# Gates as feature tiles between the attention's chunks, applied behind the outputs' transposes

## The reference

```
z = rmsnorm(x, n1) @ w_in             # 1024 -> [u | q | f | i | gate], 512 each
y_pool = (window means of u, minus u) @ w_pool * scale     # 4 groups, windows 2,4,8,16
q = silu(q) * 128**-0.5;  log_f, k from f and lb;  v = i    # 4 heads of 128
o = S-recurrence over chunks: causal part with decays + q * exp(G) @ S
o = o * rsqrt(mean(o*o) + eps) * g_norm * silu(gate)
x = x + concat(y_pool, o) @ w_out
x = x + conv_ffn(rmsnorm(x, n2));  y = final rmsnorm
```

## Time and profile before

| | us |
|---|---|
| median of 3 runs | 2874.8 (2872.68 to 2878.28) |
| the profiled execution | 2871.09 |
| its span, first to last instruction | 2869.2 |
| PE busy in the span | 2614.6 (91%) |
| DVE busy | 1202.9 (42%) |
| ACT busy | 697.0 (24%) |
| POOL busy | 440.4 (15%) |
| mean granted clock of TensorE | 0.955 of full |

### The profile page before, as it was taken

One profiled execution on the slowest core, in us unless ns is written; L12 is line 12 of the kernel. 1 busy time (PEld: TensorE's weight loads), 2 busy tenths in 40 slices (PEclk: granted clock), 3 DMA queues, 4 the chain that ended last, 5 costly groups with the idle time before them and its releaser, 6 DMA issues.

```text
span 2869.2 us, 34984 instructions
## 1 busy us (share of the span) xinstructions
PE 2614.6 (91%) x12479; PEld 2132.6 (74%) x12479; DVE 1202.9 (42%) x2344; ACT 697.0 (24%) x1389; POOL 440.4 (15%) x316
## 2 busy tenths in 40 slices
PE   5977786999889998899999998899999998899997
PEld 4865665888767787688877787688877787688776
DVE  5624844444524548422224548321224746322224
ACT  2211302222222333211122323211122422211123
POOL 3420332455545102000000002000000011000000
PEclk8986898999989999999999999899999999999999
DMA  4542023666666651355564641355555631355553
GB/s 146 192 160 88 8 97 113 225 237 220 237 224 230 254 209 45 118 185 188 188 217 181 238 173 44 121 189 190 189 221 193 246 125 60 147 190 190 209 194 137
DMA packets 142288, 489.07 MB, mean 170 GB/s; under 512 B 8897, under 2 KB 75697, under 8 KB 92840
## 3 DMA queue, kind: packets, MB, share of 16 engines
q1 hardware_dynamic: 133689, 482.67, 47.1%
q10 hardware_dynamic: 8472, 4.75, 0.6%
HBM read 375.54 MB, written 112.02 MB: 170 GB/s over the span
## 4 chain that ended last, share of the span: by engine, by line
PE 64%; DMA 8%; DVE 6%; issue 4%; ACT 2%; SPq 1%; DVEq 0%; POOL 0%; ACTq 0%
PE ps L493 20%; PE ps L495 20%; PE ps L494 20%; DMA w_split<-w_both 8%; PE ps L621 1%; DVE arena L1647 1%; PE ps L647 1%; ACT arena L972 1%; SPq L370 1%; DVE arena L1615 1%; PE ps L525 0%; DVE x_tok L1709 0%; DVE arena L1614 0%; DVE h_lo L1367 0%; DVE arena L1359 0%
## 5 line engine op out<-in xcount | busy, mean ns | idle before, releaser
L493 PE MATMUL ps<-h_hi,w_both 128*128 128x512 f32 (+1 forms) x1888 | 746.9, 396 | 19.2 <-DVE x_tok L1709 8.9
L495 PE MATMUL ps<-h_lo,w_both 128*128 128x512 f32 (+1 forms) x1888 | 739.2, 392 | 0.0
L494 PE MATMUL ps<-h_hi,w_both 128*128 128x512 f32 (+1 forms) x1888 | 736.0, 390 | 0.0
L493 PEld LDWEIGHTS ps<-h_hi,w_both 128*128 128x128 f32 x1888 | 360.7, 191 | 97.6 <-issue 21.8
L495 PEld LDWEIGHTS ps<-h_lo,w_both 128*128 128x128 f32 x1888 | 360.4, 191 | 81.5
L494 PEld LDWEIGHTS ps<-h_hi,w_both 128*128 128x128 f32 x1888 | 361.1, 191 | 78.8
L493 PE MATMUL ps<-w_both,act_hi 128*128 128x512 f32 (+1 forms) x748 | 301.2, 403 | 27.2 <-DVE act_lo L1782 27.2
L495 PE MATMUL ps<-w_both,act_hi 128*128 128x512 f32 (+1 forms) x748 | 299.2, 400 | 0.0
L494 PE MATMUL ps<-w_both,act_lo 128*128 128x512 f32 (+1 forms) x748 | 298.3, 399 | 0.0
L1782 DVE TENSOR_TENSOR act_lo<-arena,act_hi 128x512 fp32r<-128x512 f32 (+1 forms) x176 | 133.5, 762 | 342.9 <-ACT act_hi L1255 342.9
L328 POOL TENSOR_TENSOR arena<-arena 128x256 f32<-128x256 f32 x56 | 40.5, 723 | 1511.8 <-DVE arena L1615 1511.8
(11 more groups left out here) (238 smaller groups left out, 2924.0 us busy)
## 6 DMA issues: line engine op xcount, KB each, us to landing
w_both<-w_split SPq DMA_DIRECT2D x288, 1024.0 KB, 4.8
w_split<-w_both SPq DMA_DIRECT2D x96, 1024.0 KB, 6.2
w_raw<-in_w_down SPq DMA_DIRECT2D x24, 512.0 KB, 4.2
w_raw<-in_w_a SPq DMA_DIRECT2D x22, 512.0 KB, 4.3
w_raw<-in_w_b SPq DMA_DIRECT2D x22, 512.0 KB, 4.3
w_raw<-in_w_in SPq DMA_DIRECT2D x20, 512.0 KB, 4.3
x_tok<-in_x_prompt SPq DMA_DIRECT2D x16, 512.0 KB, 6.7
arena<-in_x_prompt SPq DMA_DIRECT2D x16, 512.0 KB, 5.6
```

Source lines behind the costliest of these rows:

```text
L493: nc.tensor.matmul(out, lhs[0], rhs[0], start=first, stop=False)
L494: nc.tensor.matmul(out, lhs[1], rhs[0], start=False, stop=False)
L495: return nc.tensor.matmul(out, lhs[0], rhs[1], start=False, stop=last)
```

## The change

The order of the units becomes f, q, v, u, gate. V's token tiles go to PSUM banks 4 to 7, in the place of the gates. The gates are now feature tiles of 24 matmuls (`gate_tile`), in banks 6 and 7 by turns. In blocks 1 to 3 they lie behind chunks 5, 7, 8 and 10, and u tiles 1 to 3 behind chunks 0, 2 and 4. In block 0 gate tile 0 comes ahead of the attention, the others behind chunks 2, 6 and 10, with their head rows in bank 4, which the outputs use: so PE waits there for ACT's copy (`gate_taken`) ahead of the next outputs. `u_tile(0)` now waits for ACT's copies of v (`v_taken`), since they free bank 6.

ACT copies each gate tile from PSUM over the sums of logarithms `g_t`, when the last decays have read them (`take_gate`, wait on `eg_ready`). It applies SiLU to them in place behind chunks 10 to 13, with a table load for Silu behind chunk 9 and one back behind chunk 13.

The outputs are no longer multiplied by the gate in the chunk. ACT copies them from PSUM to `o_tok`, then squares from there; PE waits for that copy alone (`o_taken`). The pooled products go behind chunks 12 to 15, in block 0 too, where their head rows (bank 4) again make PE wait for the low part (`pool_taken`) before it goes on; the output product waits for all four.

In the tail DVE scales `o_tok` by the root alone, PE transposes it, and DVE multiplies the transposes by the gain (now a column of `vec`) and the gate tile into `yg` (`gated`); ACT's high and DVE's low part read `yg`. The load of the gain over all partitions is gone.

```diff
-U_F, U_Q, U_GATE, U_V, U_U, U_OUT, U_UP, U_DOWN = 0, 4, 8, 12, 16, 20, 28, 72
+U_F, U_Q, U_V, U_U, U_GATE, U_OUT, U_UP, U_DOWN = 0, 4, 8, 12, 16, 20, 28, 72
-U_BEHIND = {g: g + 1 for g in range(HEADS - 1)}
-POOLED_BEHIND = {0: 0, 1: 1, 2: 2, 11: 3}
-PRODUCT_BEHIND = {10 + g: g for g in range(HEADS)}
-LOW_BEHIND = {11 + g: g for g in range(HEADS)}
+U_BEHIND = {0: 1, 2: 2, 4: 3}
+POOLED_BEHIND = {0: 0, 1: 1, 3: 2, 10: 3}
+GATE_BEHIND = ({5: 0, 7: 1, 8: 2, 10: 3}, {2: 1, 6: 2, 10: 3})
+SILU_BEHIND = {10: 0, 11: 1, 12: 2, 13: 3}
+PRODUCT_BEHIND = {12 + g: g for g in range(HEADS)}
+LOW_BEHIND = ({13: (0,), 14: (1,), 15: (2, 3)}, {12 + g: (g,) for g in range(HEADS)})
```

PE in `attention`, its waits ahead of a chunk's outputs, what it puts behind a chunk, and the new `gate_tile`:

```diff
-                        pe.wait_ge(o_squared, n)
-                        pe.wait_ge(o_gated, n)
+                        pe.wait_ge(o_taken, n)
+                    if hd and i == 0:
+                        pe.wait_ge(gate_taken, 1)
+                    if hd and i - 1 in GATE_BEHIND[1]:
+                        pe.wait_ge(gate_taken, GATE_BEHIND[1][i - 1] + 1)
+                    if hd and i - 1 in PRODUCT_BEHIND:
+                        pe.wait_ge(pool_taken, PRODUCT_BEHIND[i - 1] + 1)
...
+                    if i in GATE_BEHIND[hd]:
+                        gate_tile(b, hd, GATE_BEHIND[hd][i], i + 1)
+                    if i in PRODUCT_BEHIND:
+                        pool_product(b, hd, PRODUCT_BEHIND[i], i + 1)
...
+            def gate_tile(b, hd, g, chunks):
+                if g < 2:
+                    pe.wait_ge(u_taken, 4 * b + (4 if hd else 3 + g))
+                else:
+                    pe.wait_ge(gate_taken, 4 * b + g - 1)
+                feature_tile(b, U_GATE + g, g, 6 + g % 2, 4, hd, win(2 + g % 2).start, chunks)
```

PE in `body`, ahead of the attention:

```diff
-                token_tiles(b, U_GATE, (4, 5, 6, 7), 2, hd)
+                token_tiles(b, U_V, (4, 5, 6, 7), 2, hd)
...
-                token_tiles(b, U_V, (0, 1, 2, 3), 4, hd)
-                pe.wait_ge(gate_taken, 4 * b + 4)
...
-                    for g in range(HEADS):
-                        pe.wait_ge(pooled_ready, g + 1)
...
-                    pe.wait_ge(pool_taken, 4)
...
+                    gate_tile(0, 1, 0, 0)
                 attention(b, hd)
```

ACT:

```diff
+                def take_gate(g):
+                    act.wait_ge(unit_done, UNITS * b + U_GATE + g + 1)
+                    act.wait_ge(eg_ready, 4 * b + g + 1)
...
+                    nc.scalar.copy(gate_t[:, g, HEAD:WIDE], ps[:, 6 + g % 2, :]).then_inc(gate_taken, 1)
+                def silu(g):
+                    act.wait_ge(gate_taken, 4 * b + g + 1)
+                    nc.scalar.activation(gate_t[:, g, lo:WIDE], gate_t[:, g, lo:WIDE], ACT.Silu).then_inc(gate_ready, 1)
...
                     act.wait_ge(o_done, n + 1)
+                    nc.scalar.copy(o_tok[:, w, win(h)], ps[:, 4, 0:P]).then_inc(o_taken, 1)
+                    act.wait_ge(o_taken, n + 1)
...
+                    if i == min(SILU_BEHIND) - 1:
+                        nc.scalar.preload_act_table(ACT.Silu)
```

DVE in the attention and in the tail (`mixer_output`):

```diff
-                    dve.wait_ge(o_squared, n + 1)
-                    v.tensor_tensor(gt, gt, ps[:, 4, 0:P], ALU.mult).then_inc(o_gated, 1)
...
-                        last = v.scalar_tensor_tensor(out=gt, in0=gt, scalar=orstd[rows, 4 * t + h:4 * t + h + 1],
-                                                      in1=gn[rows, :], op0=ALU.mult, op1=ALU.mult)
+                        last = v.tensor_scalar(ot, ot, orstd[rows, 4 * t + h:4 * t + h + 1], None, ALU.mult)
...
+                    v.scalar_tensor_tensor(out=yg[:, t, :].rearrange("p (k n) -> p k n", k=4),
+                                           in0=ps[:, 6 + t % 2, :].rearrange("p (k n) -> p k n", k=4), scalar=gcol,
+                                           in1=gate_t[:, :, main(t)], op0=ALU.mult, op1=ALU.mult).then_inc(yg_ready, 1)
```

More of the change, by code:

```diff
@@ L201, in trunk_step @@
         g_t = part(4480, HEADS, WIDE)
-        gate = part(6720, TILES + 1, 512)
+        o_tok = part(6720, TILES + 1, 512)
+        gate_t = g_t
         v_tok = part(9280, TILES + 1, 512)
@@ L540, in feature_tile @@
                 if hd:
-                    last = features(u % 4, ps[:, bank_head, 0:HEAD], slice(0, HEAD))
+                    if o_behind:
+                        pe.wait_ge(o_taken, o_behind)
+                    last = features(u % 4, ps[:, bank_head, at:at + HEAD], slice(0, HEAD))
                 last.then_inc(unit_done, 1)
@@ L673, in u_tile, with pool_product @@
                     pe.wait_ge(u_taken, 4 * b + g - 1)
+                else:
+                    pe.wait_ge(v_taken, 4 * b + 3 + g)
                 feature_tile(b, U_U + g, g, 6 + g % 2, None, 0)
-            def pool_product(b, g):
+            def gate_tile(b, hd, g, chunks):
+                if g < 2:
+                    pe.wait_ge(u_taken, 4 * b + (4 if hd else 3 + g))
+                else:
+                    pe.wait_ge(gate_taken, 4 * b + g - 1)
+                feature_tile(b, U_GATE + g, g, 6 + g % 2, 4, hd, win(2 + g % 2).start, chunks)
+            def pool_product(b, hd, g, chunks):
                 pe.wait_ge(pooled_ready, 4 * b + g + 1)
-                if g >= 2:
+                if g < 2:
+                    pe.wait_ge(gate_taken, 4 * b + 3 + g)
+                else:
                     pe.wait_ge(pool_taken, 4 * b + g - 1)
-                nc.tensor.matmul(ps[:, 6 + g % 2, :], wp[:, g, :], pooled[:, g, HEAD:WIDE], start=True,
-                                 stop=True).then_inc(pool_done, 1)
+                last = nc.tensor.matmul(ps[:, 6 + g % 2, :], wp[:, g, :], pooled[:, g, HEAD:WIDE], start=True, stop=True)
+                if hd:
+                    at = win(2 + g % 2).start
+                    pe.wait_ge(o_taken, chunks)
+                    last = nc.tensor.matmul(ps[:, 4, at:at + HEAD], wp[:, g, :], pooled[:, g, 0:HEAD], start=True,
+                                            stop=True)
+                last.then_inc(pool_done, 1)
             def head_attention():
@@ L803, in body @@
                     if t >= 2:
[L804 removed]
+                        pe.wait_ge(yg_ready, 4 * b + t - 1)
                     for h in range(HEADS):
[L806 removed]
+                        last = nc.tensor.transpose(ps[:, 6 + t % 2, h * P:(h + 1) * P], o_tok[:, t, h * P:(h + 1) * P], ident)
                     last.then_inc(yt_done, 1)
@@ L1664, in attention @@
                                            in1=ps[:, 5, P:2 * P], op0=ALU.mult, op1=ALU.add).then_inc(s_ready, 1)
-                    gt = gate[:, w, win(h)]
-                    dve.wait_ge(o_squared, n + 1)
-                    v.tensor_tensor(gt, gt, ps[:, 4, 0:P], ALU.mult).then_inc(o_gated, 1)
-                    if not hd and i in LOW_BEHIND:
-                        pool_low(b, hd, LOW_BEHIND[i])
+                    for g in LOW_BEHIND[hd].get(i, ()):
+                        pool_low(b, hd, g)
                     if not hd and i in POOLED_BEHIND:
```

132 lines of the change are left out of this document (64 added, 68 removed).

## The result

The change made the kernel **slower**: 2887.07 us (2883.47 to 2887.8, 6 runs) against 2876.19 (2872.68 to 2880.72, 6 runs) of the kernel before, ratio 1.0033, 95% interval 1.0021 to 1.0045. That is 10.9 more; the forecast was 3.6 less, and the range ended at 2886.0.

What follows compares the result with a forecast made beforehand. The prediction took TensorE as the bound, busy for 2614.6 of 2869.2 us. Block 0's -13.5 and +9.9 for blocks 1 to 3 (+3.3 each) gave -3.6, a median of 2871.2 us, range 2857 to 2886.

Steps and rivals of the forecast that it cites:

- V's gap: Blocks 1 to 3, ahead of attention: PE idles 4.5, outputs start 17.6 us earlier, clock costs 1.6; together -16.0 a block.
- 99.2, chunk 5 in 10, chunk 10 in 10.5: Block 1's attention: expected durations in us; the attention of blocks 1 to 3 was priced at +18.0 each.
- +1.3: Tail of blocks 1 to 3: eight DVE passes instead of four delay PE's second half to 6.05 us, +1.3 a block.
- Rival 2: Slower: TensorE's clock falls to 1.2 GHz at eight more new or longer waits, 1.6 each, 2884.0 us; chance 0.17.
- -13.5: Block 0 in all: gates and v, head recurrence, stretch ahead of attention, attention and tail sum to 13.5 us less.
- Head recurrence -2.8: Block 0's four heads: DVE's wait for ACT's square and its gate multiplication go, 0.7 us each, -2.8 (0 to -8).
- Ahead of the attention -9.5: Block 0: four serial products go; transposes, gate tile 0 and copies replace them, 26.0 us instead of 35.5.
- Attention +23.2: Block 0: gate tiles behind chunks 2 and 6 +9.1 and +7.5, chunk 10 0, catch-up -4.1, products +10.7 us.
- Tail +2.1: Block 0's tail: 1.3 us for the added DVE passes and 0.8 for the head rows' serial gate pass.
- rival 4: Block 0: PE waits for gate units split by slow POOL, losing 4 to 13.5 us, 2875.2 to 2884.7; chance 0.10.
- Rival 3: The Silu table load costs more than its 1.28 us row; if double, 1.28 more at four chunks 10, 2876.3; chance 0.03.
- Rival 1: Faster: tiles fill the attention's idle in blocks 1 to 3, floor +12.5, 5.5 us less a block, 2854.7; chance 0.25.

Runs made afterwards that it cites:

- Six repairs together: Changed kernel with earlier v copies, reordered ScalarE work (attention and block 0), head-row products together, early transposes, table padded to 128 rows: 2823.24 us, ratio 0.9818 to before.

## Why the prediction was wrong

**Blocks 1 to 3: the sum right, its terms in part by luck.**
- V's gap: forecast idle 4.5, start 17.6 earlier, 1.6 of clock; measured 4.36, clock 0.59. Right, and here the clock fell in all three blocks; the run with the gap filled shows the clock's price apart from the wait's.
- Attention, "99.2, chunk 5 in 10, chunk 10 in 10.5": 97.4, 9.7 and 9.9. The waits are where they were said, by the reasons that were said (the run with the other order on ScalarE), each 0.3 to 0.6 smaller. Chunk 3's 6.0 had the same cause; I took it for the kernel's own, and it was the largest of the three, 2.8.
- Tail, "+1.3", 6.05 said and 6.12 measured. Here **the clock was left out**: it fell behind the tail in all three blocks. That its 1.6 to 2 a block made up for the attention's 1.8 is luck, and so is the last row of the table above.
- Rival 2, with a chance of 0.17, named eight new places for this. The clock fell at four: the three tails, and block 0's last product (0.59 in the 4 us behind it). Behind chunk 10's wait of 1.6 it stayed at 1.00 in all of blocks 1 to 3, and in block 0 chunk 10 holds less idle time than before (2.0, and 7.9 before).

**Block 0: -13.5 said, +6.6 measured.** The steps that failed are the head recurrence and the stretch ahead of the attention (together 8.0 over their forecast), the tail (4.5), the attention (3.3), and two terms put at nothing without a reason, the clock behind the tail (2.5) and the start (2.4):
- The start, left out of the sum and so taken at 0: 2.4 by one more row in a table. I had read this part of the change as costing nothing.
- "Head recurrence -2.8": +0.9. VectorE's saved wait is there (intervals of 25.0 are 24.1 to 24.7 now, some 2.1 in all). But PE is busy for 16.3 and not 19.3 in two of the four intervals before and in one after, as the clock falls less there, which is 3.0. In the kernel with 113 rows, otherwise like before, the same stretch took 91.3 and not 88.3. So the term was about right, and the profile before had a lucky clock.
- "Ahead of the attention -9.5": -5.2. A split of a gate unit by GpSimd stands beside VectorE's last pooling sums there now: four of them take 5.64 where they took 2.90 (rows below), and PE waits 6.45 for the state work behind them, where before 3.9. And gate tile 0 took 11.2, not 9.4. The larger point is that I priced this tile as serial with the decays and didn't ask why: the order on ScalarE made it so (13.4 in the run). Together with the head recurrence this was forecast at -12.3 and is -4.3. Against two other profiles of the order before (129.7 and 132.8, where this one has 127.7) it would be -6.3 and -9.4; the changed order takes 122.6 to 123.5 in eight profiles. So a part of this miss is the execution that was profiled before.
- "Attention +23.2": +26.5. Chunks 2 and 6 took 12.3 and 12.4 as said, the four products' stretch 21.9 (22.2 said). Chunk 10 took 14.2, 2.4 more and not 0, near the upper bound of 2.7 named there. Light chunks gave back 3.1, not 4.1.
- "Tail +2.1": +6.6, of which 2.9 because two low parts from SBUF met GpSimd's split (4.19, and 1.29 before). The earlier trace rows had shown that pairing, and rival 4 named it for another place. The other 1.6 is the clock behind the last product's wait.
- Behind the tail 0, measured +2.5. The clock in that window is 0.89 and was 0.96.

VectorE's pooling sums ahead of block 0's attention, before and after, and GpSimd's split beside the latter:

```profile
269.13 2.90 DVE L1482 TENSOR_TENSOR arena<-arena 128x526 f32<-128x526 f32 x4
```

```profile
245.33 5.64 DVE L1516 TENSOR_TENSOR arena<-arena 128x526 f32<-128x526 f32 x4
247.76 2.66 POOL L478 TENSOR_TENSOR w_both<-w_raw,w_both 128x1024 fp32r<-128x1024 f32 x1
```

Rival 3 was wrong. ACT at chunk 9 and 10 of block 1:

```profile
1128.47 1.28 ACT L1165 ACT_TABLE_LOAD   x1
1129.77 0.27 ACT L1144 COPY arena<-ps 128x128 f32<-128x128 f32 x1
```

The kd copy starts as the load ends; nothing drains, and the drain that the Trainium skill, "ScalarE: Activation LUTs", section "What ACT_TABLE_LOAD costs", gives has no row here. Rival 1 was refused by the chunks, and the reason given against it was right. Rival 4's waits for split units are not there: PE waited 0.2 for them in all.

**What stays open.** Of the 16.8 between the profiles a part is the clock at stops that the change doesn't touch (two kernels of one order differed by 3.0 in the head recurrence alone); the medians differ by 10.9 only. Which stops fall I can't say from the program; that they differ in one execution is shown. What GpSimd cost in the head recurrence and ahead of the attention was read from the traces, and wasn't tried by itself. So was chunk 10 of block 0, whose 2.4 no run takes apart. And what gate tiles are worth in block 0, against a kernel before with its block 0 repaired as well, wasn't tried.

## To carry to other kernels

Six repairs together gave no less than alone (62.5 against 56.9): none of them only laid bare another's wait. A stop of an engine that bounds the kernel costs the stop and, often, the clock behind it; count both, and compare a filler that does nothing with a repair that removes the wait. Work moved between other work is only as good as the order of the engine that takes it: here the order of copies, decays and table load on ScalarE, the place of the transposes and of the head rows' products, and one row count turned a loss of 11 us into a gain of 52. A kernel that has been repaired must be set against one whose own waits were looked for as hard. Price the block with the special cases as carefully as the loop, down to the number of rows of a small load.
